# Two transformer blocks on one core: the second block's mixer attention by pairs of heads on different halves of TensorE's array

## The reference

```python
def gqa_attend(q, k, v, sink=None):
    s = jnp.einsum('bqkgd,bjkd->bkgqj', q, k).astype(jnp.float32) * (HEAD_DIM ** -0.5)
    if sink is not None:
        sl = jnp.broadcast_to(sink.reshape(N_KV_HEADS, GQ)[None, :, :, None, None].astype(jnp.float32),
                              s.shape[:-1] + (1,))
        s = jnp.concatenate([s, sl], axis=-1)
    p = jax.nn.softmax(s, axis=-1)
    if sink is not None:
        p = p[..., :-1]
    return jnp.einsum('bkgqj,bjkd->bqkgd', p.astype(v.dtype), v)

def layer(x, xc, ...):
    ...
    ya = short_conv_mixer(a_b, a_c, a_h, conv_a)
    yb = conformer_conv(b_v, b_g, conv_b, conv_b_bias, cln_g, cln_b)
    yc = window_attention(apply_rope(q_heads(c_q), cos, sin), apply_rope(kv_heads(c_k), cos, sin),
                          kv_heads(c_v), kc_c, vc_c, sink)
    yd = global_attention(apply_rope(rms_norm_2(q_heads(d_q), qn_g), cos, sin),
                          apply_rope(rms_norm_2(kv_heads(d_k), kn_g), cos, sin),
                          kv_heads(d_v), kc_d, vc_d)
    x_new = x + g1 * (jnp.concatenate([ya, yb, yc, yd], axis=-1) @ w_out)
    h2 = rms_norm_2(x_new, n2) * (1 + sc2) + sh2
    x_new = x_new + g2 * expert_choice_ffn(h2, router, w_gate, w_up, w_down)
    if need_ctx:
        ...
        ycc = gqa_attend(q_heads(cc_q), kc_c, vc_c, sink).reshape(bsz, lc, GROUP_W)
        ycd = gqa_attend(rms_norm_2(q_heads(cd_q), qn_g), kc_d, vc_d).reshape(bsz, lc, GROUP_W)
        ...
```

## Time and profile before

| | us |
|---|---|
| median of 3 runs | 2611.3 (2608.67 to 2613.83) |
| the profiled execution | 2610.9 |
| its span in the trace, first to last instruction | 2608.7 |
| mean granted clock of TensorE over the span | 0.908 |
| TensorE (PE) matmuls busy | 2201.0 (84%) |
| VectorE (DVE) busy | 752.9 (29%) |
| ScalarE (ACT) busy | 613.6 (24%) |
| GpSimd (POOL) busy | 742.7 (28%) |
| HBM read | 633.17 MB, 243 GB/s over the span |

### The profile page before, as it was taken

How to read it: one execution, slowest core, us unless ns; L and a number is a source line. 1 busy time by engine, 2 the same in 40 slices (tenths; PEclk the granted TensorE clock), 3 DMA queues, 4 the chain that set the end, 5 groups by cost and what they waited for, 6 DMA issues and landing times.

```text
span 2608.7 us, 31087 instructions
## 1 busy us (share of the span) xinstructions
PE 2201.0 (84%) x12070; PEld 1405.0 (54%) x12070; DVE 752.9 (29%) x1432; ACT 613.6 (24%) x896; POOL 742.7 (28%) x625
## 2 busy tenths in 40 slices
PE   7988889989798899789798999999979875656664
PEld 6866778868677788635455444444347531121211
DVE  4744221122521211355553112221246520000001
ACT  3544333433643234211342000000021410000000
POOL 7736346787383477610300000000010100000000
PEclk9989989999898899899798899999999888777787
DMA  8324658654256586621101799999973049999996
GB/s 261 130 97 145 226 182 283 224 169 146 81 178 211 178 306 224 217 76 65 65 1 65 310 421 422 422 422 422 422 273 124 6 165 421 421 421 422 421 421 285
DMA packets 171519, 635.90 MB, mean 244 GB/s; under 512 B 10040, under 2 KB 16440, under 8 KB 122120
## 3 DMA queue, kind: packets, MB, share of 16 engines
q1 hardware_dynamic: 168368, 623.79, 62.0%
q0 software_dynamic: 2880, 10.29, 1.5%
q10 hardware_dynamic: 152, 0.17, 0.0%
HBM read 633.17 MB, written 1.05 MB: 243 GB/s over the span
## 4 chain that ended last, share of the span: by engine, by line
PE 65%; DMA 17%; DVE 8%; ACT 3%; issue 3%; POOL 2%; SPq 1%; DVEq 0%; ACTq 0%
PE bank L1125 14%; PE bank L508 9%; PE bank L510 9%; PE bank L509 9%; DMA ring<-in_w_up 7%; PE bank L961 5%; DMA ring<-in_w_gate 4%; DMA ring<-in_w_down 3%; PE bank L1081 3%; PE bank L1139 3%; PE bank L1149 2%; PE bank L684 2%; POOL ring_r L1282 2%; PE bank L970 2%; DMA ring<-in_ffn_w_gu 2%
## 5 line engine op out<-in xcount | busy, mean ns | idle before, releaser
L1282 POOL TENSOR_TENSOR ring_r<-ring,ring_r 128x512 fp32r<-128x512 f32 (+1 forms) x544 | 671.4, 1273 | 387.3 <-ACT ring_r L1379 325.1
L1125 PE MATMUL bank<-ring,arena 128*64 128x512 f32 (+1 forms) x3072 | 587.5, 706 | 191.9 <-DMA ring<-in_w_up 68.2
L508 PE MATMUL bank<-ring_r 128*128 128x256 f32 (+1 forms) x1504 | 471.0, 313 | 42.1 <-DVEq L1842 27.6
L1125 PEld LDWEIGHTS bank<-ring,arena 128*64 128x64 f32 (+1 forms) x3072 | 175.9, 141 | 586.1 <-issue 572.5
L510 PE MATMUL bank<-xT_r,ring_r 128*128 128x256 f32 x1248 | 359.6, 288 | 0.0
L509 PE MATMUL bank<-ring_r 128*128 128x256 f32 x1248 | 358.6, 287 | 0.0
L1379 ACT ACTIVATE ring_r<-ring 128x2048 fp32r<-128x2048 f32 (+1 forms) x138 | 253.1, 1840 | 414.3 <-PE bank L510 214.4
L508 PEld LDWEIGHTS bank<-ring_r 128*128 128x128 f32 x1504 | 295.2, 196 | 68.4 <-DVEq L1842 30.1
L510 PEld LDWEIGHTS bank<-xT_r,ring_r 128*128 128x128 f32 x1248 | 245.7, 197 | 0.0
L509 PEld LDWEIGHTS bank<-ring_r 128*128 128x128 f32 x1248 | 244.3, 196 | 0.9 <-issue 0.7
L1312 POOL TENSOR_TENSOR arena<-const 128x1024 f32<-128x1024 f32 x6 | 12.4, 2070 | 734.2 <-DVEq L1842 621.9
(11 more groups left out here) (301 smaller groups left out, 2541.0 us busy)
## 6 DMA issues: line engine op xcount, KB each, us to landing
ring<-in_w_gate SPq DMA_DIRECT2D x128, 1024.0 KB, 16.2
ring<-in_w_up SPq DMA_DIRECT2D x128, 1024.0 KB, 18.8
ring<-in_w_down SPq DMA_DIRECT2D x128, 1024.0 KB, 19.3
ring<-in_ada_w SPq DMA_DIRECT2D x48, 1024.0 KB, 6.2
ring<-in_ffn_w_gu SPq DMA_DIRECT2D x40, 1024.0 KB, 5.3
ring<-in_ffn_w_down SPq DMA_DIRECT2D x20, 1024.0 KB, 5.1
ring<-in_mem_wkv SPq DMA_DIRECT2D x16, 1024.0 KB, 5.1
ring<-in_w_in SPq DMA_DIRECT2D x16, 1024.0 KB, 14.2
```

The source lines that it names most:

```text
L508: pe.matmul(dst, w_hi, v_hi, start=first, stop=False)
L1125: mm = pe.matmul(dst[nb][W * j:W * j + W, :], src[:, 2 * q + c, W * j:W * j + W], wide_of((u0 + k) % RING)[:, c, UN * nb:UN * nb + UN], st ...
L1282: pool.tensor_tensor(lo[:, c], whole[:, c], hi_of(u)[:, c, 0:n], ALU.subtract).then_inc(*signal("w_lo", (u, c)))
```

## The change

The second block's attention goes by pairs of units. The heads are listed in the order 0, 3, 1, 2, so that the two of a pair have different key heads (their scores use different row halves of the array) and outputs on different partitions (their values use different column halves). Scores and values of a pair are interleaved matmul by matmul. A wide pair's scores fill banks 2 to 5; its transposes use 6, 1, 0 and 6 again; its values share bank 7, which VectorE reads once filled for both. Probabilities have four places, the third and fourth in `xT`, where POOL's scratch was; that moves to `xT[:, 6:8]`, on which the second kind's outputs are written, so VectorE waits for `short` before the first of them. `deep` is the distance of units that share a place. TensorE's order is now scores of pair j + 1, values of pair j - 1, transposes of pair j; ScalarE's is the exponentials of a pair, then the copies of the pair before; VectorE's is normalise, maxima of the next pair, output of the pair before. `diff_scores` interleaves its two groups.

The core of the diff:

```diff
-            return dict(key=(stage, i), n=i, ...)
+            return dict(deep=4 if size == 1024 else 2, key=(stage, i), n=i, ...)
...
         def probs_of(u):
 
+            if u["size"] == 1024 and u["n"] % 4 >= 2:
+                m = u["n"] % 4
+                return xT[:, 2 * m - 4:2 * m - 2, :].rearrange("p a b -> p (a b)")[:, 0:2 * u["keys"]].rearrange("p (a b) -> p a b", a=2)
             return area(u["n"] % 2 * u["size"], 2, u["keys"])
...
-                    for h in range(N_HEADS):
+                    for h in (0, 3, 1, 2):
...
-            stage, n = u["key"][0], u["n"] - 2
+            stage, n = u["key"][0], u["n"] - u["deep"]
...
+            def pair_scores(a, b):
+
+                parts = a["keys"] // 256
+                for part in range(parts):
+                    banks = []
+                    for m, u in enumerate((a, b)):
+                        at = 2 * part if parts == 2 else 2 * (u["n"] // 2 % 2)
+                        banks.append(open_bank(("s",) + u["key"] + (part,), 2 + at + m))
+                    for t in (range(2) if parts == 1 else [part]):
+                        for kb in range(len(a["k"])):
+                            at = 256 * (t if parts == 1 else kb)
+                            for u, bk in zip((a, b), banks):
+                                mm = pe.matmul(bk[:, at:at + 256], u["q"][0][:, t * P:t * P + P], u["k"][kb][0], start=True, stop=True)
+                                if (kb == len(a["k"]) - 1) and (parts == 2 or t == 1):
+                                    mm.then_inc(*filled_now(("s",) + u["key"] + (part,)))
+
+            def pair_turn(a, b):
+
+                for m, u in enumerate((a, b)):
+                    pe.wait_ge(*after("probs", u["key"]))
+                    pr = probs_of(u)
+                    for part in range(u["keys"] // 256):
+                        key = ("pT",) + u["key"] + (part,)
+                        bk = open_bank(key, (6, 1, 0)[m + part if u["keys"] == 256 or m == 0 else 2 - 2 * part])
...
+                        mm.then_inc(*filled_now(key))
+
+            def pair_values(a, b):
+
+                for u in (a, b):
+                    pe.wait_ge(*after("probsT", u["key"]))
+                o = open_bank(("o",) + b["key"], 7)
+                n = a["keys"] // P
+                for kb in range(n):
+                    for u in (a, b):
+                        p0 = u["y"][0][1]
+                        mm = pe.matmul(o[p0:p0 + 64, 0:256], u["v"][kb], probsT_of(u)[:, kb, :], start=(kb == 0), stop=(kb == n - 1))
+                mm.then_inc(*filled_now(("o",) + b["key"]))
+
+            def attend_pairs(us):
+
+                pairs = list(zip(us[0::2], us[1::2]))
+                pair_scores(*pairs[0])
+                for j in range(len(pairs) + 1):
+                    if j + 1 < len(pairs):
+                        pair_scores(*pairs[j + 1])
+                    if j:
+                        pair_values(*pairs[j - 1])
+                    if j < len(pairs):
+                        pair_turn(*pairs[j])
...
                     def diff_scores(u):
...
+                        h = u["n"]
+                        banks = [open_bank(("s",) + u["key"] + (m,), (4, 2)[h % 2] + m) for m in range(2)]
+                        for t in range(2):
+                            for m in range(2):
...
-                attend(us)
+                attend_pairs(us)
...
-                    tmp = xT[:, i, 0:SEQ * seqs].rearrange("p (s k) -> p s k", k=SEQ)
+                    tmp = xT[:, 6 + i, 0:SEQ * seqs].rearrange("p (s k) -> p s k", k=SEQ)
...
-                if u["n"] >= 2:
+                if u["n"] >= u["deep"]:
                     act.wait_ge(*full(turned(u)))
...
+            def attend_pairs(us):
+
+                for j in range(0, len(us) + 2, 2):
+                    for u in us[j:j + 2]:
+                        exps(u)
+                    for u in us[max(j - 2, 0):j]:
+                        evac_T(u)
...
-                if u["n"] >= 2:
+                if u["n"] >= u["deep"]:
                     dve.wait_ge(*full(turned(u)))
...
+            def pair_output(a, b):
+
+                key = ("o",) + b["key"]
+                dve.wait_ge(*full(key))
+                for u in (a, b):
+                    y, p0 = u["y"][0]
+                    ins = dve.tensor_copy(y, bank_of(key)[p0:p0 + 64, 0:256])
+                link(ins)
+                drop(key)
+                done("oT", b["key"])
+
+            def attend_pairs(us, second_kind):
+
+                pairs = list(zip(us[0::2], us[1::2]))
+                for u in pairs[0]:
+                    maxima(u)
+                for j in range(len(pairs) + 1):
+                    if j < len(pairs):
+                        for u in pairs[j]:
+                            normalise(u)
+                    if j + 1 < len(pairs):
+                        for u in pairs[j + 1]:
+                            maxima(u)
+                    if j == 3:
+                        second_kind()
+                    if j:
+                        pair_output(*pairs[j - 1])
...
-                attend(block2_units(layer))
+                attend_pairs(block2_units(layer), lambda: dve.wait_ge(*after("short", layer)))
```

More of the change, by code:

```diff
@@ L395, in unit @@
         def unit(stage, i, q, k, scale, v, y, keys=256, bias=None, sink_at=None, size=512, parts=None):
-            return dict(key=(stage, i), n=i, q=q, k=k, scale=scale, v=v, y=y, keys=keys, bias=bias, sink=sink_at, size=size, parts=parts)
+            return dict(deep=4 if size == 1024 else 2, key=(stage, i), n=i, q=q, k=k, scale=scale, v=v, y=y, keys=keys, bias=bias, sink=sink_at, size=size, parts=parts)
         def half(t, c, j, n0=0, n=SEQ):
@@ new lines, in pair_turn @@
+            def pair_turn(a, b):
[5 more added lines that the diff above has]
+                        bk = open_bank(key, (6, 1, 0)[m + part if u["keys"] == 256 or m == 0 else 2 - 2 * part])
+                        for kb in range(2):
+                            for t in range(2):
+                                mm = pe.transpose(bk[:, 256 * kb + P * t:256 * kb + P * t + P],
+                                                  pr[:, t, (2 * part + kb) * P:(2 * part + kb + 1) * P], ident)
+                        mm.then_inc(*filled_now(key))
@@ L832, in diff_scores @@
                     def diff_scores(u):
-                        for m in range(2):
-                            h = u["n"]
-                            b = open_bank(("s",) + u["key"] + (m,), (4, 2)[h % 2] + m)
-                            for t in range(2):
-                                mm = pe.matmul(b[:, 256 * t:256 * t + 256], half(qT, h, m)[:, t * P:t * P + P],
+                        h = u["n"]
+                        banks = [open_bank(("s",) + u["key"] + (m,), (4, 2)[h % 2] + m) for m in range(2)]
+                        for t in range(2):
+                            for m in range(2):
+                                mm = pe.matmul(banks[m][:, 256 * t:256 * t + 256], half(qT, h, m)[:, t * P:t * P + P],
                                                half(kT, h, m), start=True, stop=True)
-                            mm.then_inc(*filled_now(("s",) + u["key"] + (m,)))
+                                if t == 1:
+                                    mm.then_inc(*filled_now(("s",) + u["key"] + (m,)))
                     def value_rows(u):
@@ L1467, in evac_T @@
                 if u["n"] >= 2:
-                    act.wait_ge(*full(("o", u["key"][0], u["n"] - 2)))
+                    act.wait_ge(*full(("o", u["key"][0], u["n"] - 2 if u["deep"] == 2 else u["n"] // 2 * 2 - 1)))
                 for part in range(u["keys"] // 256):
@@ L1793, in _ @@
                     done("yb", (layer, c))
-                attend(block2_units(layer))
+                attend_pairs(block2_units(layer))
                 for k in range(2 * len(tiles)):
```

## The result

The changed kernel takes **2626.9 us** (median of four runs, 2625.8 to 2631.6), the kernel before 2611.3 in the same comparison: ratio 1.0063, 95% interval [1.0046, 1.0081]. That is 15.6 us slower, above the forecast of 2613.5 and outside its range. The profiled execution took 2625.8 with a span of 2624.0, against 2608.7.

What follows compares the result with a forecast made beforehand. TensorE was taken to bound the attention stages, with expert weights waiting behind them. Savings of -7.6 us and clock charges of +10.2 gave +2.6 on 2610.9, so 2613.5 us, range 2604 to 2620.

Steps and rivals of the forecast that it cites:

- the drain: Uncovered end of each attention stage: 9.0 us in layer 0; in layer 1, with two wide rings, 22.4 against 24.6, -2.2.
- The late return of the clock: TensorE reaches the unbiased scores still at 0.50 after some 10 us without work: +2.4 in each layer, +4.8.
- its later falls: Gaps of about 2 us in the wide rings let the clock fall to 0.50: 1.5 in each layer, +3.0.
- Times are counted from the first scores: Starting point of the attention stage forecast, 2022.95 in layer 1; no cost was given for anything ahead of it.
- The start to the first exponential without bias: Biased heads opening each attention stage: 29.0 us against 29.7 in layer 1, -0.7 in each layer before clock charges.
- The wide ring: Period of an unbiased wide pair in the attention, bank 6 step included: 7.9 us against 9.64, -1.7 a pair.
- The narrow heads: Layer 0's eight narrow heads up to the output projection: 28.6 us before, some 27 in pairs, -1.
- The output projection at 0.50: Gaps at the stage's end start the projection at half clock: up to 1.7, taken as 1.2 in each layer, +2.4.
- side by side: Two heads share the array in halves: a wide pair's scores 2.0 us, values 1.9, TensorE's work 9.64 to 6.0.
- differential scores: Interleaved score matmuls of the first block's attention: 0, at worst a few tenths.
- the clock stays down: Rival, chance 0.20: wide pairs run at 0.50, a wide step costs +2.4 instead of -1.7; 2624, or 2620 us.
- The halves don't overlap: Rival, chance 0.05: a pair's scores take 4.0 and values 3.8, about 8 us more in each layer; 2627 us.

Runs made afterwards that it cites:

- with bank 7: Changed kernel with the second head's second transposes of a wide pair in bank 7 instead of bank 6; 2612.6 us, ratio 1.0005.
- the new drain: Last pair's transposes moved ahead of the values before it, into free score banks, on the changed kernel with both bank edits; 2600.8 us.
- the last version: Changed kernel with first scores in banks 4 and 5, last transposes in bank 7, and last pair's transposes ahead of earlier values; 2600.8 us, ratio 0.9963.
- the run with 9: Changed kernel with 9 unused 128x512 matmuls in TensorE's 10.4 us gap, writing bank 7; 2625.7 us, ratio 1.0053.

## Why the prediction was wrong, step by step

**The step that failed** is the sum of waits at the two ends of a stage. The walk had nothing for the time until the first scores find their banks empty, and it sized the last pairs' steps and the drain (9.0 us in layer 0, -2.2 in layer 1) without laying out in what order copies, values and transposes stand there. In its place the runs show 2.5 us of TensorE waiting for ScalarE ahead of the first scores in each layer, and in layer 1's drain 5.0 us of ScalarE waiting for transposes behind the values. With other banks for the first scores and bank 6, and the last transposes ahead, the stages took 125.2 us for 146.5.

Put piece by piece against the ledger, with the clock charges where they were made, the forecast missed 12.7 of the span's +15.3 us: 5.1 ahead of the first scores; -2.3 from there to the first exponential without bias (+3.4 forecast in the two layers, +1.1 measured); 1.9 in layer 0's wide pairs (-1.5, +0.4); 4.8 in the narrow heads (-1, +3.8); 2.2 behind the first unbiased exponential of layer 1 (-0.7, +1.5); 1.0 outside the stages (+2.4, +3.4). The late return of the clock was near in size. For its later falls I took +3.0; the rows named below that ran at 0.50 were 7.6 us longer by it (1.4, 0.7, 2.7 and 2.8), and how much of that lay on the path no run shows.

- **"Times are counted from the first scores"** was the step that lost the start: I took the first scores to come as before and never asked who holds the banks that they open. Missing: +2.5 of waiting in each layer. Undoing the start of it made the stages 1.3 to 2.2 a layer shorter, and 1.1 to 1.4 with bank 7 beside it.
- **The start to the first exponential without bias**: -0.7 and +2.4 for the late clock, +1.7 in each layer; measured -0.2 and +1.3. No part of the loss against the forecast lies here. But the walk read the 10 us without work only as a matter of clock. I wrote that the next scores stand behind the bank 6 transposes and still let them wait for free; with bank 7 the same piece is 2.8 and 3.5 us shorter.
- **The wide ring**: 7.9 forecast, 8.2 measured in layer 1 (2064.98 to 2073.21), -1.4 for -1.7. In layer 0 the rings were 9.9 and 8.8, and two wide pairs and the step to the narrow ones took +0.4 for -3.0: the fourth pair's scores took 3.4 us there for 2.0, and the last wide values 2.7 for 1.95, since the clock fell twice. Each ring held 2.3 us of waiting for bank 6, which the 7.9 had in it.
- **The narrow heads**: the term that was mis-sized most, -1 forecast, +3.8 measured. I had three steps of 7.6, 6.0 and 4.5 and a drain of 9.0, some 27 us; from exponential to exponential they took 8.2, 6.3, 6.8 and 11.2. The third step's values, transposes and scores (layer 0, changed kernel) stand behind a wait for ScalarE's copies and ran at 0.50, 6.0 us for 3.3:

```profile
1335.80 1.97 PE L730 MATMUL bank<-arena 128*64 128x256 f32 x8 [2.98 <-ACTq L1474]
1337.70 1.97 PE L717 MATMUL bank<-const,xT 128*128 128x128 f32 x8
1339.60 2.08 PE L703 MATMUL bank<-arena 64*128 64x256 f32 x8
```

  With bank 7 the same rows came at 1.00, behind a shorter wait:

```profile
1333.72 1.08 PE L730 MATMUL bank<-arena 128*64 128x256 f32 x8 [2.13 <-ACTq L1474]
1334.73 1.09 PE L717 MATMUL bank<-const,xT 128*128 128x128 f32 x8
1335.76 1.13 PE L703 MATMUL bank<-arena 64*128 64x256 f32 x8
```

  There the steps are 7.3, 6.3 and 4.8 and the drain 11.2, 29.6 together; with the new drain that is 9.0 and the whole 27.8. So the sizes that I had for the steps and the drain are nearly those of a kernel whose waits are moved. That the third step's 2.0 us are the clock's alone isn't shown, since the edit changed the waits as well.
- **The drain in layer 1**: -2.2 for everything behind the first unbiased exponential, +1.5 for one fall of the clock; measured +1.5. From the last pair's first exponential to the output projection it took 18.0 us (2073.21 to 2091.20), in which ScalarE waits 5.0 for transposes that stood behind the values, and values and transposes at 0.50 take 2.8 more than at full clock (3.68 + 3.01 for 1.95 + 1.97); the two overlap. I had named the drain as uncovered and didn't lay its order out.
- **The output projection at 0.50**: +1.2 in each layer. In layer 0 its first records lost 2.45 us, of which 0.2 were left 103 us later; in layer 1 nothing, whose first 7 us hold the 17 records of before. The kernel's time has no cost of it that is shown.
- **Readings**: the walk books -1 where 28.6 less 27.1 is 1.5, and takes 18.4 and 24.6 for 18.2 (1301.12 to 1319.35) and 24.7 (2052.63 to 2077.37). Together that is 0.4 us.
- **What held**: TensorE stopped being the bound; side by side is real at the sizes read from the earlier trace rows; differential scores cost nothing that can be measured, and VectorE didn't wait for POOL in either stage; the clock was back for the unbiased pairs 28.3 and 31.5 us after the first scores; the stages' +11.9 and, in the last version, -9.5 us came out at the end of the kernel as +15.3 and -10.2 of span, which agrees with what I read from the earlier trace rows to within the scatter outside the stages.

Of the rivals, "the clock stays down" had the nearest time with the wrong mechanism: the clock was down in pieces, and keeping it up at the third pair's scores in layer 1 gave 2.3 us. "The halves don't overlap" named 2627, but they do.

The Trainium skill's warning, "TensorEngine Tiling (Array Packing)", section PSUM Bottleneck, that evacuation rather than TensorE may bound a packed kernel, deserved more weight than I gave it, in another form than I worked out: ScalarE's throughput wasn't the limit (44.96 us busy of 85.76), but when it emptied a bank was. The page speaks of a fourfold speed-up, and the pairs here are two by two. By throughput the traces don't bear it out; that the emptying of PSUM came to decide they do, by TensorE's 28 us of waits for ScalarE in layer 0's stage.

## What to carry to other kernels

When units are grouped, each group opens more banks at once and gives them back later. For every bank that the new order opens, write down who has to empty it, where that instruction stands in its engine's queue, and what is queued behind the opening; do it for the first group and the last one too, where the pattern of the middle doesn't hold. Work saved on an engine that then waits is no gain until the waits are moved: here 32 us less of TensorE's work made the kernel 15.6 us slower, and other banks for two groups and another place for the last transposes turned that into 10.5 us faster than before.

## What the runs showed of the hardware

- One matmul of 128x512 in 32-bit floats stands in the trace as two records: 14 issued gave 28, 9 gave 18, 0.44 us a record at full clock (7.89 / 18, layer 0 of the run with 9).
- After 7.9 us of unbroken matmuls a gap of 2.70 us was followed by work at 0.50, and after 9.6 us a gap of 1.02 by work at 1.00. These are one case each; behind a gap of 2.80 us in the first block the clock stayed at 1.00.
- The granted clock changed twelve times in the 86 us of layer 0's stage, six rises and six falls, with TensorE's gaps of 0.5 to 3.6 us and one of 10.4; before, it rose once in that stage and stayed.
- A start at 0.50 didn't last as a loss here: the 2.45 us by which layer 0's output projection was late at its 21st record had shrunk to 0.2 at the 321st. Between them the clock's longest stretch at 0.50 was 17.1 us for 23.9 in the kernel before.
